# Two transformer blocks on one core: the expert gather spread over the stages of the second mixer

## The chip, the cores and the metric

One core of one Trainium2 chip runs the whole program. The metric is device time in microseconds, the median of repeated executions. Everything is float32 in memory, 512 tokens, model width 1024.

## The reference

Two blocks follow each other on `x`. Each is a token mixer and then a PEER feed-forward, in which every token picks 128 rows (8 heads, 16 each) of two tables of 16384 experts:

```python
def peer_ffn(h, ...):
    s1, s2 = scores of the two halves of q = h @ w_query against 128 keys each
    v1, i1 = top_k(s1, 16); v2, i2 = top_k(s2, 16)
    top_v, pos = top_k(v1[:, None] + v2[None, :], 16)      # 16 of 256
    expert_idx = i1 * 128 + i2 at pos;  gates = softmax(top_v)
    act = gelu(einsum('d,kd->k', h, expert_down[expert_idx]))
    return einsum('k,kd->d', gates * act, expert_up[expert_idx])

def second_block(x, mem, ...):
    h = rmsnorm(x); z = h @ w_in                           # 47 chunks of 128 columns
    o_fox = causal attention, 8 heads of 64, with a forget term cumsum(log_f) over all tokens before
    o_swa = window attention, 8 heads of 64, window 128, ALiBi, sinks
    o_mem = attention to 256 memory rows, 4 heads of 128   # keys and values from mem alone
    merged = sum of sigmoid(gates_i) * (o_i @ w_o_i)
    x = x + merged @ w_out
    x = x + peer_ffn_2(rmsnorm(x))
```

The second mixer of a token reads that token's `x` after the first feed-forward, and keys and values of the tokens before it, never after it.

## The kernel before

The program is a sequence of stages, each a block in which every engine has its own instruction list; at the end of a block all engines meet at a barrier. Activations lie feature-major in SBUF (`xT`, `hT`: 128 x 8 x 512). The order inside a stage is written by hand, with semaphores; nothing is scheduled by a planner.

- **First mixer** (from the start to about 1005 us), untouched but for the layout of two weights. Then norm `n2` and `peer` for the first feed-forward ("e1").
- **`peer`** (L1230) is `project_stage` for the queries (`e1q`, 16 chunks) and `sparse_stage` (L1050 on). `project_stage` (L261) takes a chunk of weights (512 KB), splits it on ACT and DVE into a high and a low part, and makes 24 products of 128x128 by all the tokens on TensorE. Two weight buffers, four PSUM banks.
- **`sparse_stage`**: for a tile of 128 tokens DVE chooses the experts in 21 pieces (`choose`, L1158). The gather then runs over 512 **slots**, 4 tiles of 128 experts. For a slot POOL issues one indirect DMA (L1064) of 128 rows of 8 KB, the down row and the up row of one expert per token side by side (1 MB) into one of 8 `pair` buffers. DVE takes the dot product of the down half with `hrow` (L1219). After every 4 slots ACT takes gelu (`bent`), DVE multiplies by the gate (`weight`), ACT makes a diagonal matrix per slot (`diag`, L1131), and TensorE adds `diag` times the up half into two banks (L1101, L1102). A buffer is free when TensorE is done (`added`), and POOL waits for that before it issues the slot that is 8 later. The choosing of tile t+1 is spread over the slots of tile t; that of tile 0 stands alone ahead of the gather.
- **Second mixer** (`second_mixer`, L1373), all 512 tokens at once, nothing beside it: norm `n3`; projection `p2` of 47 chunks; head norms `hn`; `forget`; `vt` (values turned); the attentions `foxa`, `swaa` (with a load of ALiBi first), the memory path (`mn`, `mp`, `mh`, `mt`) and `mema`; `mg2` (`merge_stage`, L960); `po2`; norm `n4`.
- **Second feed-forward** ("e2"), the same as the first: queries, choosing of tile 0, 512 slots, and the store of `xT`.

`attention_stage` (L502) works item by item (a head and a tile of queries): TensorE scores, DVE takes the peak, ACT exponentiates, DVE scales, TensorE turns, ACT copies, TensorE weighs the values, DVE takes the output, each a step or more behind the other, with 3 PSUM banks for scores and 2 for outputs. `norm_stage` (L224), `head_norm_stage` (L1238), `turn_stage`, `forget_stage` are short chains over ACT, TensorE and DVE. What sets the order around the change:

```python
for n in range(N):                                   # POOL, sparse_stage
    t, s = divmod(n, NJ)
    if s == 0:
        pool.wait_ge(chosen, t + 1)
    if n >= BUFS:
        pool.wait_ge(added, n - BUFS + 1)
```

Of the kernel before, what the change touches and what calls it, by code (L numbers as in the profile page):

```python
# [14 lines left out]
P = 128  # L15
S = 512
# [19 lines left out]
Y_FQ, Y_FK, Y_FV, Y_SQ, Y_SKV, Y_MQ, Y_GATE, Y_FF, Y_N = 0, 4, 8, 12, 16, 18, 22, 46, 47  # L36
# [138 lines left out]

class AdaBeside:
# [47 lines left out]
def norm_stage(nc, name, k, src, chunks, width, gain, dst, shift=None, tokens=S):  # L224

    with ExitStack() as stack:
# [4 lines left out]
        with nc.Block() as block:  # L231
            @block.scalar
            def _(act):
                for c in range(chunks):
                    act.activation(sq[:, c, :], src[:, c, :], ACT.Square).then_inc(sq_ready, 1)
                act.wait_ge(mean_ready, 1)
                act.activation(root[:], mean[:], ACT.Sqrt).then_inc(root_ready, 1)

            @block.tensor
            def _(pe):  # L240

                for c in range(chunks):
                    pe.wait_ge(sq_ready, c + 1)
                    last = pe.matmul(ss[:, 0:tokens], k.ones[:], sq[:, c, :], start=c == 0, stop=c == chunks - 1)
                last.then_inc(ss_ready, 1)

            @block.vector
            def _(dve):
                link = Chain(dve, chain)
                dve.wait_ge(ss_ready, 1)  # L250
# [3 lines left out]
                for c in range(chunks):  # L254
                    ins = dve.scalar_tensor_tensor(dst[:, c, :], src[:, c, :], gain[:, c:c + 1], rstd[:], ALU.mult, ALU.mult)
                    if shift is not None:
                        link(ins)
                        dve.tensor_scalar(dst[:, c, :], dst[:, c, :], shift[:, c:c + 1], None, ALU.add)


def project_stage(nc, name, k, w_dram, act_in, kc, chunks, dst, tokens=S, add=None, parts=None, ada=None):  # L261
# [4 lines left out]

    with ExitStack() as stack:
        r = Room(nc, stack, name)
        hhi, hlo = parts or (r.sb("hhi", [P, kc, tokens], F32R), r.sb("hlo", [P, kc, tokens], F32R))
# [4 lines left out]
        turns = (chunks - 1) // 4  # L274
# [12 lines left out]
        with nc.Block() as block:  # L287
            @block.sync
# [11 lines left out]
            def _(act):  # L300
# [7 lines left out]
                loop(act, body)  # L308

            @block.tensor  # L310
            def _(pe):
                def body(n, q, i):
# [9 lines left out]
                    if beside and q == 3 and i is not None:  # L322
                        beside.product(pe, i)

# [7 lines left out]
            def _(dve):  # L332
# [4 lines left out]
                def body(n, q, i):  # L337
                    if not (isinstance(n, int) and n == chunks - 1):
                        split_w(n + 1, q + 1)
                    if beside and i is not None:  # L340
                        beside.sums(dve, i, q)
                    dve.wait_ge(made, n + 3)
# [17 lines left out]
                if beside:  # L360
                    beside.finish(dve)

# [139 lines left out]
def attention_stage(nc, name, k, items, heads, vdim, oT, sinks=None):  # L502
# [5 lines left out]
    N = len(items)  # L508
    with ExitStack() as stack:
# [5 lines left out]
        ps = [r.ps(f"ps{u}") for u in range(3)]  # L515
        pt = [r.ps(f"pt{u}") for u in range(2)]
        po = [r.ps(f"po{u}") for u in range(2)]
# [3 lines left out]
        with nc.Block() as block:  # L521
            @block.tensor
            def _(pe):
                def score(n):
                    q_ap, k_ap, more = items[n][0], items[n][1], items[n][6]
                    if n >= 3:
                        pe.wait_ge(exped, n - 2)
                    out = ps[n % 3][:, 0:width[n]]
# [13 lines left out]
                def weigh_values(n):  # L542
                    vs, at = items[n][3], (items[n][4] % per) * vdim
                    pe.wait_ge(copied, n + 1)
                    if n >= 2:
                        pe.wait_ge(taken, n - 1)
                    for j, v in enumerate(vs):
                        last = pe.matmul(po[n % 2][at:at + vdim, 0:P], v, pT[n % 2][:, j * P:(j + 1) * P],
# [3 lines left out]
                for step in range(N + 3):  # L552
# [4 lines left out]
                    if 3 <= step:  # L557
                        weigh_values(step - 3)

            @block.scalar  # L560
            def _(act):
                for step in range(N + 2):
                    if step < N:
# [4 lines left out]
                        act.activation(p[n % 3][:, 0:width[n]], ps[n % 3][:, 0:width[n]], ACT.Exp, bias=nmax[:, n:n + 1],  # L568
# [5 lines left out]
                    if step >= 2:  # L574
# [4 lines left out]
                        act.activation(pT[n % 2][:, 0:width[n]], pt[n % 2][:, 0:width[n]], ACT.Copy).then_inc(copied, 1)  # L579

            @block.vector
            def _(dve):
                link = Chain(dve, chain)
                masked = [0]

                def peak(n):
# [3 lines left out]
                    if bias is not None:  # L590
                        part = ps[n % 3][:, w - bias.shape[-1]:w]
# [1012 lines left out]
```

## Time and profile before

| | |
|---|---|
| median of 3 runs | 5064.99 us (5050.13 to 5074.23) |
| the profiled execution: its time, its span | 5070.55 us, 5068.7 us |
| busy: PE, DVE, ACT, POOL | 75%, 54%, 16%, 23% of the span |
| DMA | 1194.16 MB, of them 1073.81 MB by the gather's queue |
| first gather, second gather | 1170 to 2607 us, 3627 to 5062 us |
| between them (second mixer, queries, choosing of tile 0) | 2607 to 3627 us |

The profile gives busy time per engine, a picture of the span in 40 slices, the costliest groups of instructions (line, engine, operation, tiles written and read, count, busy time, mean, idle time before them and what ended it), and DMA sizes with the time from issue to landing. Tile names have their buffer numbers left out. A float32 product on TensorE shows as two records. The granted clock is given as a share of 2.4 GHz: 1.00 is 2.4 GHz, 0.50 is 1.2 GHz.

### The profile page before, as it was taken

The page shows a single profiled execution, that of the slowest core. Times are in us where ns is not written, and L with a number is a line of the kernel's source. Part 1 is how long each engine was busy: PE and PEld are TensorE (multiplying, and loading weights), DVE is VectorE, ACT ScalarE, POOL GpSimd, SP SyncE. Part 2 cuts the span into 40 slices and gives each one's busy share as a digit, 9 for nine tenths or more (in the row PEclk, how much of TensorE's full clock was granted, in tenths as well). Part 3 has the DMA queues.
Part 4 walks back from the last instruction along what each step waited for, and adds up shares of the span by engine and source line. Part 5 has one row for each costly group of instructions (what it writes and reads, how often), then busy time and mean ns, then how long its engine had stood idle before and what let it go on. Part 6 is the DMA issues. An engine that isn't in the chain of part 4 may idle for free. (4 is left out here: it accounts for less than half of the span.)

```text
span 5068.7 us, 35703 instructions
## 1 busy us (share of the span) xinstructions
PE 3812.7 (75%) x11658; PEld 2123.6 (42%) x11658; DVE 2712.9 (54%) x5846; ACT 813.6 (16%) x2074; POOL 1174.9 (23%) x1028
## 2 busy tenths in 40 slices
PE   5945897775677777677779979788477777777777
PEld 4823796462233233233338734546223332322333
DVE  5558555346655656644443334533665565565454
ACT  1113001111111111111121212322111111111111
POOL 0000000002443444344410000000144334434443
PEclk9978787887888998888889955699788888988898
DMA  4500000127999999999952200122399999999998
GB/s 173 181 16 3 4 1 21 56 64 282 366 376 368 369 393 368 360 387 395 394 212 95 73 1 9 42 75 75 147 365 363 387 352 373 383 357 381 400 414 344
DMA packets 198993, 1194.16 MB, mean 236 GB/s; under 512 B 21642, under 2 KB 44426, under 8 KB 64914
## 3 DMA queue, kind: packets, MB, share of 16 engines
q0 software_dynamic: 147456, 1073.81, 53.3%
q1 hardware_dynamic: 51124, 118.42, 7.1%
q8 instruction: 76, 1.25, 0.1%
q14 instruction: 81, 0.66, 0.0%
q10 hardware_dynamic: 256, 0.02, 0.0%
HBM read 1190.04 MB, written 2.10 MB: 235 GB/s over the span
## 5 line engine op out<-in xcount | busy, mean ns | idle before, releaser
L1064 POOL DMA_INDIRECT e1g_pair<-in_experts,e1g_expert x512 | 585.7, 1144 | 1997.7 <-DVE e1g_expert L1196 1169.8
L1064 POOL DMA_INDIRECT e2g_pair<-in_experts,e2g_expert x512 | 589.0, 1150 | 1865.9 <-DVE e2g_expert L1196 1043.4
L1219 DVE CUSTOM_DVE_ANT_0 e2g_pair<-e2g_pair,e2g_hrow 128x1024 f32<-128x1024 f32 x512 | 626.4, 1225 | 601.6 <-DMA e2g_pair<-in_experts,e2g_expert 601.2
L1219 DVE CUSTOM_DVE_ANT_0 e1g_pair<-e1g_pair,e1g_hrow 128x1024 f32<-128x1024 f32 x512 | 626.8, 1225 | 598.8 <-DMA e1g_pair<-in_experts,e1g_expert 598.1
L1101 PE MATMUL e1g_acc<-e1g_pair,e1g_diag 128*128 128x512 f32 x1024 | 616.7, 688 | 425.2 <-ACT e1g_diag L1131 425.0
L1101 PE MATMUL e2g_acc<-e2g_pair,e2g_diag 128*128 128x512 f32 x1024 | 618.5, 689 | 422.7 <-ACT e2g_diag L1131 422.4
L1102 PE MATMUL e1g_acc<-e1g_pair,e1g_diag 128*128 128x512 f32 x1024 | 579.9, 651 | 0.0
L1102 PE MATMUL e2g_acc<-e2g_pair,e2g_diag 128*128 128x512 f32 x1024 | 579.0, 650 | 0.0
L1101 PEld LDWEIGHTS e1g_acc<-e1g_pair,e1g_diag 128*128 128x128 f32 x1024 | 210.1, 217 | 743.5 <-ACT e1g_diag L1131 460.1
L1101 PEld LDWEIGHTS e2g_acc<-e2g_pair,e2g_diag 128*128 128x128 f32 x1024 | 210.1, 217 | 739.6 <-ACT e2g_diag L1131 456.6
L1102 PEld LDWEIGHTS e2g_acc<-e2g_pair,e2g_diag 128*128 128x128 f32 x1024 | 219.2, 214 | 294.5 <-issue 294.5
L1102 PEld LDWEIGHTS e1g_acc<-e1g_pair,e1g_diag 128*128 128x128 f32 x1024 | 218.6, 213 | 293.3 <-issue 293.3
L318 PE MATMUL p_ps<-p_hhi,p_whi 128*128 128x512 f32 x648 | 255.4, 394 | 38.8 <-DVE p_wlo L335 38.8
L319 PE MATMUL p_ps<-p_hlo,p_whi 128*128 128x512 f32 x648 | 254.0, 392 | 0.0
L320 PE MATMUL p_ps<-p_hhi,p_wlo 128*128 128x512 f32 x648 | 253.9, 392 | 0.0
L1125 ACT ACTIVATE e2g_bent<-e2g_dot 128x4 f32<-128x4 f32 x128 | 26.3, 205 | 1053.8 <-DVE e2g_dot L1219 1053.8
L1125 ACT ACTIVATE e1g_bent<-e1g_dot 128x4 f32<-128x4 f32 x128 | 26.3, 205 | 1052.8 <-DVE e1g_dot L1219 1052.8
L1131 ACT ACTIVATE e1g_diag<-held_ident,e1g_weight 128x128 f32<-128x128 f32 x512 | 163.6, 390 | 165.0 <-DVE e1g_weight L1225 164.8
L1131 ACT ACTIVATE e2g_diag<-held_ident,e2g_weight 128x128 f32<-128x128 f32 x512 | 163.6, 390 | 164.8 <-DVE e2g_weight L1225 164.6
L345 DVE COPY mix_z<-p_ps 128x512 f32 (+1 forms) x81 | 56.0, 691 | 232.4 <-PE p_ps L320 232.4
L318 PEld LDWEIGHTS p_ps<-p_hhi,p_whi 128*128 128x128 f32 x648 | 122.8, 190 | 65.8 <-issue 40.5
L304 ACT ACTIVATE p_whi<-p_raw 128x1024 fp32r<-128x1024 f32 x81 | 85.8, 1061 | 352.8 <-PE p_ps L320 349.0
(515 smaller groups left out, 4704.5 us busy)
## 6 DMA issues: line engine op xcount, KB each, us to landing
p_raw<-in_w_in SPq DMA_DIRECT2D x81, 512.0 KB, 3.5
p_w_ada<-in_w_ada SPq DMA_DIRECT2D x16, 1024.0 KB, 6.1
ada_w<-in_w_ada SPq DMA_DIRECT2D x4, 2048.0 KB, 10.6
po_raw<-in_w_out SPq DMA_DIRECT2D x16, 512.0 KB, 3.6
e1q_raw<-in_w_query SPq DMA_DIRECT2D x16, 512.0 KB, 3.5
e1g_pair<-in_experts,e1g_expert POOLq DMA_INDIRECT x512, 9.0
e2q_raw<-in_w_peer_q SPq DMA_DIRECT2D x16, 512.0 KB, 3.5
e2g_pair<-in_experts,e2g_expert POOLq DMA_INDIRECT x512, 8.9
```

The lines of the kernel that those rows point to most:

```text
L304: act.activation(whi[q % 2][:], raw[q % 2][:], ACT.Copy).then_inc(w_hi, 1)
L318: pe.matmul(out, hi, hhi[:, c, :], start=c == 0, stop=False)
L319: pe.matmul(out, hi, hlo[:, c, :], start=False, stop=False)
L320: last = pe.matmul(out, lo, hhi[:, c, :], start=False, stop=c == kc - 1)
L345: ins = dve.tensor_copy(row(dst, n), got)
L1064: pool.indirect_dma_start(pair[n % BUFS][:], None, table, bass.IndirectOffsetOnAxis(ap=expert[:, t % 2, s:s + 1], axis=0)).then_inc(landed ...
L1101: pe.matmul(acc[0][:], diag[n % DIAGS][:], pair[n % BUFS][:, D:D + 512], start=s == 0, stop=s == NJ - 1)
L1102: pe.matmul(acc[1][:], diag[n % DIAGS][:], pair[n % BUFS][:, D + 512:2 * D], start=s == 0, stop=s == NJ - 1).then_inc(added, 1)
L1125: act.activation(bent[:, t % 2, at], dot[:, t % 2, at], gelu).then_inc(bent_made, 1)
L1131: act.activation(diag[n % DIAGS][:], k.ident[:], ACT.Copy, scale=weight[:, t % 2, s:s + 1]).then_inc(diag_made, 1)
L1219: ins = dve.tensor_tensor_reduce(pair[n % BUFS][:, 0:D], pair[n % BUFS][:, 0:D], hrow[:, t, :], 1.0, 0.0, ALU.mult, ALU.add, dot[:, t % 2, ...
```

## The change

The gather of both layers becomes one object, `Gather`, that lives through both feed-forwards and the second mixer. Its work is written as **beats**: at beat n POOL issues the down rows of slot n+6 and the up rows of slot n-15, DVE takes the dot of slot n, ACT makes `diag` of slot n-20, TensorE adds slot n-21. Down and up rows come from two tables, by two gathers of 128 rows of 4 KB (512 KB each), into 6 buffers of each kind; a down buffer is free after the dot, an up buffer after TensorE. Gelu and gate are taken for 16 slots at a time, not 4.

Every stage from then on takes `beats` and, on each engine, puts its share of the beats between its own instructions. The tokens go by halves of 256: tiles 0 and 1 of layer 1 (beats 0 to 283) run beside the choosing of tiles 1 to 3 and the memory path, whose keys and values are parked in DRAM; then half 0 goes through the second mixer, its queries and the choosing of its first tile beside 223 beats of tiles 2 and 3 (283 to 506); the choosing of its second tile stands beside 33 beats (506 to 539); half 1 goes through the same beside 223 beats of layer 2, tiles 4 and 5 (539 to 762); its last choosing stands beside 48 beats, and `drain_stage` runs the other 241. Projections that host beats are written out flat and not as a loop, `w_in_2`, `w_out_2`, the output weights of the branches and `w_peer_q` are read once per half, the projection to gates (`pg`, 24 chunks) is split from that to the heads (`p2`, 23 chunks), and attention has 2 banks for scores and 1 for outputs. Keys, values and the running forget sum of half 0 are kept (`Past`).

```diff
+GROUP, UBUFS, VBUFS, DIAGS = 16, 6, 6, 8
+BENT_AT = GROUP + 1
+WEIGH_AT = BENT_AT + 1
+DIAG_AT = WEIGH_AT + 2
+UP_AT = DIAG_AT + 1
+BEATS = SLOTS + UP_AT + 6
+class Gather:
+    def pool(self, pool, n):
+        for m in range(0 if n == 0 else n + UBUFS, n + UBUFS + 1):
+            if m < SLOTS:
+                t, s = divmod(m, NJ)
+                if s == 0:
+                    pool.wait_ge(self.chosen, t + 1)
+                if m >= UBUFS:
+                    pool.wait_ge(self.dotted, m - UBUFS + 1)
+                pool.indirect_dma_start(self.down[m % UBUFS][:], None, self.layers[t // TT][0],
...
+        m = n - UP_AT + VBUFS
+        if 0 <= m < SLOTS:
+            t, s = divmod(m, NJ)
+            if m >= VBUFS:
+                pool.wait_ge(self.added, m - VBUFS + 1)
+            pool.indirect_dma_start(self.up[m % VBUFS][:], None, self.layers[t // TT][1],
...
+    def pe(self, pe, n):
+        m = n - UP_AT
+        if 0 <= m < SLOTS:
+            t, s = divmod(m, NJ)
+            pe.wait_ge(self.up_in[m % VBUFS], 16 * (m // VBUFS) + 16)
+            pe.wait_ge(self.diag_made, m + 1)
...
+class Beats:
+    def at(self, i):
+        return range(self.first + i * self.count // self.points, self.first + (i + 1) * self.count // self.points)
...
-def project_stage(nc, name, k, w_dram, act_in, kc, chunks, dst, tokens=S, add=None, parts=None, ada=None):
+def project_stage(nc, name, k, w_dram, act_in, kc, chunks, dst, tokens=S, add=None, ada=None, beats=None):
...
-        turns = (chunks - 1) // 4
+        turns = 0 if hosting else (chunks - 1) // 4
...
+                    if hosting:
+                        beats.pe(pe, n)
...
+                    if hosting:
+                        beats.dve(dve, n)
                     dve.wait_ge(made, n + 3)
...
+    SC, PO = (2, 1) if hosting else (3, 2)
...
-        ps = [[r.ps(f"ps{i}_{u}") for u in range(2)] for i in range(nb)]
+        ps = [r.ps(f"ps{u}") for u in range(5)]
...
+MIXER_LENGTHS = {"n3": 15, "p2": 100, "hn": 40, "vt": 8, "forget": 15, "foxa": 110, "swaa": 70, "mema": 30, "pg": 110, "mg": 70, "po": 35,
+                 "n4": 15, "q": 70, "choose": 90}
...
+        beats = shared_out(gather, 0, half_done, {"choose1": 62, "mn": 8, "mp": 50, "mh": 12, "mt": 4, "choose": 144})
...
+    starts = [half_done, first_layer_done]
+    ends = [TT * NJ - UBUFS, (TT + HTILES) * NJ - UBUFS]
+    for half in range(2):
+        t = TT + HTILES * half
+        beats = shared_out(gather, starts[half], ends[half], MIXER_LENGTHS)
+        second_mixer(nc, k, ins, cols, past, xT, hT, memory, half, beats)
...
+            project_stage(nc, f"e2qh{half}", k, ins["w_peer_q"], h, DC, 2 * PH, qT, tokens=HALF, beats=beats["q"])
...
+    drain_stage(nc, gather, Beats(gather, ends[1] + 48, BEATS))
```

How the order of instructions moves, at three places. POOL in the middle of a gather, before (`e1g_pair` are the buffers of 8 KB rows, `e1g_expert` the chosen indices):

```order
L1064 DMA e1g_pair2<-in_experts1,e1g_expert 128x2048 [waits e1g_added]
L1064 DMA e1g_pair3<-in_experts1,e1g_expert 128x2048 [waits e1g_added]
L1064 DMA e1g_pair4<-in_experts1,e1g_expert 128x2048 [waits e1g_added]
L1064 DMA e1g_pair5<-in_experts1,e1g_expert 128x2048 [waits e1g_added]
L1064 DMA e1g_pair6<-in_experts1,e1g_expert 128x2048 [waits e1g_added]
```

And after the change:

```order
L221 DMA held_up1<-in_up1,held_expert 128x1024 [waits held_added]
L214 DMA held_down5<-in_down1,held_expert 128x1024 [waits held_dotted]
L221 DMA held_up2<-in_up1,held_expert 128x1024 [waits held_added]
L214 DMA held_down0<-in_down1,held_expert 128x1024 [waits held_dotted]
L221 DMA held_up3<-in_up1,held_expert 128x1024 [waits held_added]
L214 DMA held_down1<-in_down1,held_expert 128x1024 [waits held_dotted]
```

POOL issues two gathers where it issued one, half of them waiting for DVE's dot and half for TensorE.

TensorE in the fox attention, before (`foxa_ps` scores, `foxa_pt` turned weights, `foxa_po` outputs; all heads and tiles, one item after another):

```order
L529 MATMUL foxa_ps2<-mix2_z 128x512
L531 MATMUL foxa_ps2<-fox_fk,held_hT 128x512
L539 MATMUL foxa_pt1<-held_ident,foxa_p0 128x128 x2
L548 MATMUL foxa_po0<-foxa_pT0,local_v 64x128
L529 MATMUL foxa_ps0<-mix2_z 128x128
L531 MATMUL foxa_ps0<-fox_fk,held_hT 128x128
```

And after (half 0):

```order
L743 MATMUL foxah0_ps1<-foxh0_fk,foxh0_fq 128x128
L751 MATMUL foxah0_pt1<-held_ident,foxah0_p1 128x128 x2
L760 MATMUL foxah0_po0<-foxah0_pT0,held_v 64x128 x2
L241 MATMUL held_acc0<-held_up2,held_diag6 128x512
L242 MATMUL held_acc1<-held_up2,held_diag6 128x512
L241 MATMUL held_acc0<-held_up3,held_diag7 128x512
L242 MATMUL held_acc1<-held_up3,held_diag7 128x512
L741 MATMUL foxah0_ps0<-held_fox_k,partsh0_z 128x256
L743 MATMUL foxah0_ps0<-foxh0_fk,foxh0_fq 128x256
```

One or two slots of the gather stand between two steps of the attention.

DVE inside a gather of the kernel before, where a group of four dots ends in one product with the gates:

```order
L1219 ISA e1g_pair0,e1g_dot<-e1g_pair0,e1g_hrow 128x1024
L1219 ISA e1g_dot 128x1
L1219 ISA e1g_pair1,e1g_dot<-e1g_pair1,e1g_hrow 128x1024
L1219 ISA e1g_dot 128x1
L1219 ISA e1g_pair2,e1g_dot<-e1g_pair2,e1g_hrow 128x1024
L1219 ISA e1g_dot 128x1
L1219 ISA e1g_pair3,e1g_dot<-e1g_pair3,e1g_hrow 128x1024
L1219 ISA e1g_dot 128x1
L1225 TENSOR_TENSOR e1g_weight<-e1g_bent,e1g_gate 128x4
```

And DVE in the gate projection of half 0 after the change (`pgh0_wlo` the low part of a weight chunk, `mix2h0_z` its result):

```order
L539 COPY mix2h0_z<-pgh0_ps1 128x256
L527 TENSOR_TENSOR pgh0_wlo1<-pgh0_raw1,pgh0_whi1 128x1024
L286 ISA held_down0,held_dot<-held_down0,held_hrow 128x1024
L286 ISA held_dot 128x1
L539 COPY mix2h0_z<-pgh0_ps2 128x256
L527 TENSOR_TENSOR pgh0_wlo0<-pgh0_raw0,pgh0_whi0 128x1024
L286 ISA held_down1,held_dot<-held_down1,held_hrow 128x1024
L286 ISA held_dot 128x1
L286 ISA held_down2,held_dot<-held_down2,held_hrow 128x1024
```

A dot, which waits for its gather, now stands ahead of the copy that frees a bank of the projection.

## Rows read from the trace of the kernel before

**Rows 1.** The page's picture of the span in 40 slices

```profile
PE   5945897775677777677779979788477777777777
PEclk9978787887888998888889955699788888988898
DMA  4500000127999999999952200122399999999998
```

**Rows 2.** Busy time by stage: window, its length, then as the first line says

```profile
core 0: us, PE busy (x) PEld busy (x) DVE busy (x) ACT busy (x) POOL busy (x), PEclk, DMA share, GB/s
1107.00:1170.00 63.00, 9.77 (x64) 8.61 (x64) 52.98 (x210) 7.22 (x11) 0.00 (x0) 0.61 0.01 3
1170.00:2607.00 1437.00, 1057.60 (x2176) 443.15 (x2176) 807.68 (x1811) 202.81 (x658) 585.67 (x512) 0.87 0.94 374
...
2620.00:2890.00 270.00, 255.36 (x1115) 211.22 (x1116) 101.63 (x110) 53.95 (x55) 0.00 (x0) 0.96 0.29 91
2890.00:2950.00 60.00, 47.69 (x83) 15.93 (x81) 22.32 (x44) 11.21 (x18) 0.00 (x0) 0.69 0.02 5
2950.00:2974.00 24.00, 4.50 (x20) 4.13 (x20) 10.22 (x12) 4.45 (x5) 0.00 (x0) 0.50 0.01 1
2974.00:3126.00 152.00, 150.21 (x368) 75.01 (x368) 52.88 (x193) 31.73 (x97) 0.00 (x0) 0.50 0.00 0
...
3137.00:3216.00 79.00, 77.22 (x223) 41.73 (x223) 57.03 (x238) 29.02 (x119) 0.00 (x0) 0.50 0.00 1
...
3241.00:3266.00 25.00, 24.85 (x192) 24.58 (x192) 11.66 (x15) 6.47 (x7) 0.00 (x0) 0.93 0.41 127
...
3284.00:3306.00 22.00, 20.24 (x119) 14.96 (x117) 16.42 (x70) 12.70 (x43) 0.00 (x0) 0.97 0.01 1
3306.00:3405.00 99.00, 87.49 (x200) 39.47 (x201) 34.85 (x50) 21.25 (x35) 0.00 (x0) 0.93 0.27 80
...
3563.00:3627.00 64.00, 9.95 (x64) 8.78 (x64) 52.27 (x209) 7.22 (x11) 0.00 (x0) 0.60 0.05 17
```

**Rows 3.** Waits inside the first gather (total us, times, longest)

```profile
POOL e1g_pair L1064 <- PE e1g_acc L1102: 800.3, 433, 11.3
DVE e1g_pair L1219 <- DMA e1g_pair<-in_experts,e1g_expert: 598.1, 455, 6.1
```

**Rows 4.** Timeline, first gather at full clock: start, length, what

```profile
2300.97 1.23 DVE L1219 CUSTOM_DVE_ANT_0 e1g_pair<-e1g_pair,e1g_hrow 128x1024 f32<-128x1024 f32 x1 [1.22 <-DMA e1g_pair<-in_experts,e1g_expert]
2301.37 1.02 PE L1101 MATMUL e1g_acc<-e1g_pair,e1g_diag 128*128 128x512 f32 x2
...
2302.12 0.08 DVE L1219 DVE_READ_ACCUMULATOR2_ANT e1g_dot<- 128x1 f32 x1
...
2303.09 1.02 PE L1101 MATMUL e1g_acc<-e1g_pair,e1g_diag 128*128 128x512 f32 x2
...
2303.44 1.23 DVE L1219 CUSTOM_DVE_ANT_0 e1g_pair<-e1g_pair,e1g_hrow 128x1024 f32<-128x1024 f32 x1 [1.23 <-DMA e1g_pair<-in_experts,e1g_expert]
...
2303.53 1.95 POOL L1064 DMA_INDIRECT e1g_pair<-in_experts,e1g_expert  x1 [0.52 <-PE e1g_acc L1102]
```

**Rows 5.** Timeline, POOL at the start of the first gather

```profile
1174.12 0.93 POOL L1064 DMA_INDIRECT e1g_pair<-in_experts,e1g_expert  x1 [0.30 <-issue]
```

**Rows 6.** The page's groups: count, busy us, mean ns, idle before

```profile
L1064 POOL DMA_INDIRECT e2g_pair<-in_experts,e2g_expert x512 | 589.0, 1150 | 1865.9 <-DVE e2g_expert L1196 1043.4
L1219 DVE CUSTOM_DVE_ANT_0 e2g_pair<-e2g_pair,e2g_hrow 128x1024 f32<-128x1024 f32 x512 | 626.4, 1225 | 601.6 <-DMA e2g_pair<-in_experts,e2g_expert 601.2
```

**Rows 7.** DMA issues: count, KB each, median us from issue to landing

```profile
p_raw<-in_w_in SPq DMA_DIRECT2D x81, 512.0 KB, 3.5
p_w_ada<-in_w_ada SPq DMA_DIRECT2D x16, 1024.0 KB, 6.1
e1g_pair<-in_experts,e1g_expert POOLq DMA_INDIRECT x512, 9.0
```

**Rows 8.** Busy time in the first mixer's attention, columns as in rows 2

```profile
384.00:445.00 61.00, 54.15 (x294) 34.04 (x293) 48.18 (x178) 28.61 (x90) 0.00 (x0) 1.00 0.00 1
```

More of the change, by code:

```diff
@@ L176, with shared_out @@
+def shared_out(gather, first, last, lengths):
+    whole, run, got = sum(lengths.values()), 0, {}
+    for name, length in lengths.items():
+        a, run = run, run + length
+        got[name] = Beats(gather, first + (last - first) * a // whole, first + (last - first) * run // whole)
+    return got
 class AdaBeside:
@@ L499, in _, with attention_stage @@
                 dve.tensor_copy(kk[:, :, :, NOPE:QH], bcast(kr[:], MH, 2)).then_inc(heads, 1)
-def attention_stage(nc, name, k, items, heads, vdim, oT, sinks=None):
+def attention_stage(nc, name, k, items, heads, vdim, oT, sinks=None, loads=(), beats=None):
     per = P // vdim
     N = len(items)
+    hosting = beats is not None
+    SC, PO = (2, 1) if hosting else (3, 2)
+    apart = PO == 2 or all(items[n][4] % per != items[n + 1][4] % per for n in range(N - 1))
+    beats = (beats or Beats()).over(N + 4)
     with ExitStack() as stack:
@@ L1228, in _ @@
[L1228 to L1239 removed]
+                        link(dve.tensor_tensor(gather.gate[:, t % TT, :].rearrange("p (h n) -> p h n", h=PH), tv[:], bcast(total[:], K16, 2), ALU.mult))
@@ new lines, in choose, with drain_stage, _ @@
+                        link.announce(dve.scalar_tensor_tensor(gather.expert[:, t % TT, :], found[:, 0, :], float(NK), found[:, 1, :], ALU.mult, ALU.add), gather.chosen, t + 1)
+                dve.wait_ge(loaded, 32)
+                for j, (t, _) in enumerate(tiles):
+                    for i in range(PIECES):
+                        choose(j, t, i)
+                        beats.dve(dve, PIECES * j + i)
+def drain_stage(nc, gather, beats):
+    beats = beats.over(1)
+    with nc.Block() as block:
+        @block.gpsimd
+        def _(pool):
+            beats.pool(pool)
+            gather.settle(pool)
+        @block.tensor
+        def _(pe):
+            beats.pe(pe, 0)
+        @block.scalar
+        def _(act):
+            beats.act(act, 0)
+        @block.vector
+        def _(dve):
+            beats.dve(dve, 0)
@@ L1245, in head_norm_stage @@
+def head_norm_stage(nc, name, row_pick, chunks, tokens=S, beats=None):
     N = len(chunks)
+    beats = (beats or Beats()).over(2 * N)
     with ExitStack() as stack:
@@ L1293, in _ @@
                 ins.then_inc(ones_ready, 1)
-                for n, (_, gain, _, times) in enumerate(chunks):
+                for n, (_, gain, _, times, _) in enumerate(chunks):
                     ins = dve.tensor_scalar(gains[:, n:n + 1], gain, times, None, ALU.mult)
                 link(ins)
+                for n in range(N):
+                    beats.dve(dve, n)
                 dve.wait_ge(summed, N)
```

601 lines of the change are left out of this document (369 added, 232 removed).

## Prediction

> **What bounds the kernel now.** I read the picture of the span first. DMA stands at nine tenths in two blocks of slices and at nought to three between them, and TensorE is at seven tenths or more in nearly all slices from the first gather on [rows 1]. So the two gathers are limited by moving rows, and the second mixer between them by something else. The busy times by stage say by what: a gather moves 374 GB/s with DMA at 0.94 [rows 2], 1437 us for 512 slots, 2.81 us a slot, while the projection `p2` keeps TensorE busy 255 of 270 us with DMA at 0.29. The waits inside the gather show the ring at work: POOL waits 800 us for TensorE to free a `pair` buffer, and DVE waits 598 us for rows to land [rows 3]. In the timeline rows land every 2.47 us when the queue is full (dots at 2300.97 and 2303.44), and TensorE takes 1.72 us a slot at full clock (2301.37 to 2303.09) [rows 4]. From the first gather's start (1170 us) to the end, TensorE has about 1024 x 1.72 = 1760 us of gather work and DMA at least 1024 x 2.47 = 2530 us, beside 1020 us in which nothing is gathered (2607 to 3627). The change puts these side by side. What it can win is at most that 1020 us, less what the two then cost each other.
>
> **The change part by part.** I cost the program by its stages, since beats are dealt out to stages and no stage can borrow from another: a stage takes the longest of TensorE, DVE and POOL on its own work and its beats.
>
> *POOL.* It issues 2048 gathers and not 1024. One takes 0.93 to 0.94 us, and 0.30 us pass to the next, when nothing disturbs it [rows 5], 1.24 in all. The mean is 1.15 [rows 6]: the gather at 2303.53 took 1.95 and ended 0.81 after the end of the dot that ran beside it (2303.44 + 1.23) [rows 4], so an issue that meets a running dot waits for its end. With as many dots per slot and twice the issues the mean should hold: 1.15 + 0.30 = 1.45 us an issue, 2.90 a slot. That is more than the 2.81 of now. The bound below is 1.24, where dots and issues fall into step (the rows' landing rate, 2.47 / 2, allows it too); I take 1.45, a mean over 512 issues.
>
> *DMA.* The same bytes in half the piece. A row of 4 KB in a gather is not in this trace. The nearest rows are loads of 512 KB and 1 MB, alone, 3.5 and 6.1 us to landing [rows 7]: two for one is 7.0 to 6.1, 15% more. But a gather takes 9.0 us to land while rows land every 2.47, so the fixed part is hidden by those in flight, and 12 of the new pieces are in flight. I take no cost, and 15% as the other end. The page "DMA: Bandwidth & Descriptors" of the Trainium skill (Bandwidth) says to batch to 1 MiB or more for 75% of peak, and fits one DMA as 2.0 us plus bytes by 436 GB/s: 4.4 us for 1 MiB, 6.4 for two halves, which would make a slot 4.1 us, an estimate. By that, the sum below would be about 5380. The trace speaks against it, as gathers overlap.
>
> *Weights twice.* 71 chunks of 512 KB and the output weights go once per half. At half of 3.5 us each [rows 7], as two are under way at a time, they are some 125 us per half, in stages in which TensorE sets the time; with 223 x 2.47 = 551 us of rows that is 676, below the 884 found next. No cost; were TensorE not the bound, DMA would be late next.
>
> *A mixer half.* TensorE's own work for 256 tokens: a chunk is 25 / 8 = 3.1 us (the memory projection, 8 chunks of 256 tokens) against 5.7 for 512 (270 / 47) [rows 2]. So `p2` 23 chunks 72, `pg` 75, queries 16 chunks 50, `po` 25. The attentions ran at 1.2 GHz (0.50 granted) though TensorE was busy 150 of 152 us [rows 2]; the first mixer's ran at 1.00 [rows 8]. With full 128x128 products of the gather for over half of the time I take full clock: `foxa` 152 us, halved for the tokens and halved for the clock, 38, `swaa` 20, `mema` 10; merge 87 x 0.93 / 2 = 41; head norms 48 x 0.69 / 2 = 17. The beats are dealt by the table, 223 / 778 = 0.287 a unit, at 1.72 us each on TensorE: `p2` 28.7 beats 49, `hn` 20, `foxa` 31.5 beats 54, `swaa` 34, `mema` 15, `pg` 54, merge 34, `po` 17, queries 34. Sums, with 3 to 5 us for a stage's start and end and more where a step's chain runs over three engines: `p2` 125, `pg` 133, queries 88, `po` 46, `foxa` 105, `swaa` 68, `mema` 35 (its keys come back from DRAM first), merge 80, `hn` 38; the norms 14 each, `vt` 8, `forget` 25 of the 24 it and `vt` now take together (small moves beside full queues). Choosing is DVE's: 63 us for 53 busy [rows 2], and 25.8 beats x 1.31 (a dot of 1.225 [rows 6] and its read of 0.08 [rows 4]) = 34, with the keys' load 105. In all **884 us a half**. POOL's 223 x 2.90 = 647 is hidden under it.
>
> *The rest.* Until beat 283 POOL issues 289 down and 268 up gathers, 557 x 1.45 = 808; the choosing of three tiles (190 us of DVE with the chains) and the memory path (68 us before, between 3216 and 3284) are hidden under that, with 12 us for two loads that host no beats. The choosing of tile 5: 63 + 33 x 1.31 = 106, say 110. From beat 762 on 256 down and 277 up gathers are left, 533 x 1.45 = 773, and 20 us for the last group of 16 on TensorE, the turning and the store. A projection written out flat, the norm's extra branches, barriers of blocks that were there before: no cost, hidden by TensorE's queue; the new layouts of output weights and five banks in the merge lie where DMA is at 0.27 [rows 2], no cost or gain.
>
> *Sum.* 1170 + 808 + 12 + 884 + 110 + 884 + 773 + 20 = **4661 us** of span, against 5068.7, so 408 less. The profiled execution took 5070.55 us, 0.1% over the median of 5065. I forecast 4660 for the median.
>
> **The rivals.** *A, POOL in step.* If issues take 1.24 us, the 1090 issues that lie where POOL sets the time cost 0.21 less each: 4430. For it: the down gather is issued right after a dot ends. Against: the up gather follows it and meets the next dot.
>
> *B, the slow clock stays.* If `foxa` and `swaa` still run at 1.2 GHz, they take 184 and 108 us, 119 more a half: 4900. For it: products with 64 rows and with 2 rows stay among the work, and 0.50 was granted at 99% busy.
>
> *C, small pieces cost.* 15% on 2.81 is 3.23 us a slot, 1.61 an issue: 1090 x 0.16 = 175 more, 4835. The skill's rule names a larger price, given above, and shares this case's chance.
>
> *D, the other side: lockstep.* The engines' lists are in order. A dot that waits for its rows holds the copy behind it that frees a bank; TensorE then waits at the next chunk, its own slots come late, `added` comes late, and POOL issues late. If this goes round, hosted work and gather add and do not overlap. A half then takes of its own half of 888 (2607 to 3563 without the memory path), 15 for products at 256 tokens and 64 for choosing, and 647 of gather, 1170; tile 5 takes 160, tile 7 64 more, and the first phase 257 more: 5600. It decides from the point where 410 of these 940 us are lost, an overlap under 56%. For it: one bank for outputs, two for scores, six buffers, and the last wait named for DVE in the gather is DMA [rows 3]. Against: in mixer stages TensorE needs 5.3 us for a chunk and its 1.25 slots, and POOL only 3.6, so rows should lie ready.
>
> *E, nothing.* The order lists show the beats in every stage, so the change does what it says; gains and losses could still cancel.
>
> **How the numbers follow.** The forecast has 0.55, A 0.11, B 0.10, C 0.08, D 0.13, E 0.03. A measurement of this kernel tells about 0.5% from no change. Faster is forecast, A, B and C and a part of D with partial overlap: 0.86; within 0.5% 0.03; slower 0.11. The forecast's own spread is the stage starts and chains, some 30 us in each half and 0.1 us on 1090 issues, 4530 to 4800. The range takes in A and B, 4430 to 4940, and leaves out D, E and tails of A and B.
>
> **What would show it.** In the changed profile: no stretch with DMA under half from 1170 us on; POOL's gathers at 1.1 to 1.2 us mean and 2.9 us a slot in the drain; each mixer half near 884 us with TensorE over 85% busy; a clock near 1.00 in `foxa`; the first phase ended near 1990 us. If POOL's idle time before a gather in the drain is long and ended by DMA landing through DVE, C is right; if in `p2` TensorE waits for the low part or for rows in every chunk, D is. The prediction is wrong if the halves are not near 884 or the drain is not near 2.9 a slot.

## The result, and the profile after

The changed kernel takes 5109 us (median of 5 runs, 5105.24 to 5115.27) against 5071 for the kernel before on the same chip (5 runs, 5050.13 to 5084.15): a ratio of 1.0082, 95% interval 1.0054 to 1.0109. It is slower by 0.8%, where 4660 us was forecast, and lies outside the range of 4430 to 4940. The profiled execution has a span of 5113.4 us, 452 above the sum of 4661.

The page's picture of the span of the changed kernel, to be laid beside [rows 1]:

```profile
PE   5945898773585676697689675697879685677777
POOL 0000000005665777555544356554544346777775
PEclk9977787887897999898899898898989898899999
DMA  4500000117896999787788777786778777899998
```

The hole of [rows 1] is gone: from slice 10 on DMA is at six tenths or more everywhere, so the gathers do run beside the mixer. But DMA is at seven and eight tenths where the gathers of before had nine, and TensorE, which the sum held to be over 85% busy in the mixer halves, is often at six or seven. The busy times by stretch say the same (core 0; window, its length, then PE, PEld, DVE, ACT and POOL busy with their instructions, granted clock, DMA share, GB/s). The stretches are the first phase, half 0 up to its queries, the choosing of tiles 4 and 5, half 1 up to its queries, and the end, each from block end to block end:

```profile
1173.00:2108.00 935.00, 583.79 (x1392) 238.61 (x1392) 527.22 (x1277) 123.63 (x329) 650.12 (x557) 0.89 0.88 320
2108.00:3011.00 903.00, 713.76 (x3106) 457.49 (x3106) 467.31 (x968) 230.17 (x533) 434.57 (x394) 0.89 0.80 280
3011.00:3250.00 239.00, 133.82 (x324) 57.34 (x324) 174.96 (x548) 28.64 (x75) 150.20 (x118) 0.86 0.77 268
3250.00:4179.00 929.00, 741.60 (x3226) 469.13 (x3226) 477.29 (x963) 238.79 (x533) 425.94 (x394) 0.89 0.78 272
4179.00:5113.00 934.00, 636.06 (x1340) 235.86 (x1340) 460.19 (x1019) 122.74 (x343) 649.82 (x585) 0.94 0.90 333
```

Forecast were 820, 779, 215, 779 and 898 (each half of 884 less its choosing of 105, which goes with tile 5's 110). So every stretch is too long (by 115, 124, 24, 150 and 36), most of all those with many stages. Yet *inside* a stage nothing is wrong. The same view inside `p2`, `foxa` and `pg` of half 0, `foxa` of half 1, and the end:

```profile
2140.00:2254.00 114.00, 114.00 (x658) 87.34 (x656) 66.87 (x102) 31.71 (x51) 62.87 (x54) 0.99 0.93 339
2364.00:2452.00 88.00, 84.87 (x253) 37.68 (x252) 58.23 (x155) 25.74 (x82) 67.27 (x55) 0.98 0.91 315
2606.00:2731.00 125.00, 125.00 (x708) 94.83 (x707) 75.20 (x119) 34.73 (x57) 69.38 (x61) 0.98 0.92 341
3511.00:3619.00 108.00, 107.31 (x350) 47.77 (x348) 63.88 (x155) 32.36 (x82) 62.25 (x56) 1.00 0.77 259
4480.00:5050.00 570.00, 405.50 (x813) 139.85 (x812) 251.05 (x418) 74.73 (x214) 426.66 (x402) 0.98 0.97 369
```

TensorE is busy for 114 of 114 us, 125 of 125, 107 of 108; the clock is at its upper level, 2.4 GHz, in the attentions too, and the end issues 402 gathers in 570 us, 2.84 us a slot. Lockstep (D) and the slow clock (B) cannot be seen. The time must lie where stages meet. The timeline over the end of `p2` and the start of `hn` in half 0 (start, length, what, idle before and its releaser):

```profile
2253.51 1.02 PE L242 MATMUL held_acc<-held_up,held_diag 128*128 128x512 f32 x2
...
2254.34 0.94 POOL L214 DMA_INDIRECT held_down<-in_down,held_expert  x1 [0.30 <-issue]
2255.58 0.94 POOL L221 DMA_INDIRECT held_up<-in_up,held_expert  x1 [0.30 <-issue]
2263.94 0.25 SPq L1426 DMA_DIRECT2D hnh_pick<-in_row_pick  x1
2263.95 0.73 ACT L1433 ACTIVATE hnh_sq<-partsh_z 128x256 f32<-128x256 f32 x2 [19.97 <-PEq L466]
2264.02 0.19 DVE L1460 MEMSET hnh_ones<- 128x68 f32 x2 [12.45 <-PEq L466]
...
2264.59 2.77 PE L1445 MATMUL hnh_mean<-hnh_sq,hnh_ones 128*34 128x256 f32 x6 [10.06 <-DVE hnh_ones L1466]
...
2267.11 1.68 POOL L214 DMA_INDIRECT held_down<-in_down,held_expert  x1 [10.59 <-DVE held_dot L286]
```

POOL's last gather of the block is issued at 2256.52. Then no engine does anything until 2263.9, when all start together. The releaser named is the sequencer at the barrier. The trace has one instruction on POOL in that time, a DRAIN from 2254.58 to 2263.69, which no view of the page counts as busy. The windows around it, the last 8 us of `p2`, the gap and the 8 us behind it:

```profile
2246.50:2254.50 8.00, 8.00 (x37) 4.81 (x35) 3.13 (x6) 0.00 (x0) 3.82 (x5) 1.00 0.74 247
2256.50:2263.70 7.20, 0.00 (x0) 0.00 (x0) 0.00 (x0) 0.00 (x0) 0.02 (x1) 0.68 0.48 170
2263.70:2272.00 8.30, 7.33 (x17) 2.61 (x17) 7.82 (x34) 3.29 (x9) 3.12 (x2) 0.66 0.33 92
```

In the gap only DMA works, at 170 GB/s, and it moves the gathers that were in flight. Behind it the gather's buffers have to fill again (92 GB/s). Of such block ends the changed kernel has 36 from the first gather on (6, 13, 2, 13 and 2 in the five stretches). At none of the 36 is a packet of the gather's queue still moving when the DRAIN ends; the last one has ended 0.5 to 4.6 us before (2.7 us here). POOL stands in its drain alone for 4.8 to 10.0 us each time, 240 us in all, and all engines idle for 292 us at these ends. In the kernel before the same DRAIN takes 0.03 us at its block ends in the second mixer, where nothing is in flight.

POOL's groups of the page, which answer to [rows 6], and the waits of the end stretch (4480 to 5050; total us, times, longest), which answer to [rows 3]:

```profile
L214 POOL DMA_INDIRECT held_down<-in_down,held_expert x1024 | 1140.3, 1114 | 2196.1 <-SPq L1271 1172.6
L221 POOL DMA_INDIRECT held_up<-in_up,held_expert x1024 | 1170.4, 1143 | 583.9 <-PE held_acc L242 351.3
```

```profile
PEld held_acc L241 <- DMA held_up<-in_up,held_expert: 288.1, 175, 3.2
DVE held_down L286 <- DMA held_down<-in_down,held_expert: 285.3, 179, 4.4
...
POOL held_down L214 <- issue: 61.3, 201, 0.3
POOL held_up L221 <- issue: 38.1, 125, 0.3
POOL held_up L221 <- PE held_acc L242: 25.9, 68, 3.0
```

A gather takes POOL 1.114 and 1.143 us, as forecast (1.15). In the end stretch POOL is busy 427 of 570 us, 99 more are its step of 0.30 us between issues, it waits 26 for TensorE, and the profile puts 18 down as remote; TensorE and DVE wait for rows to land. Whether the rows are late because DMA is full (0.97) or because POOL issues them late, this view does not tell. The runs e10 and e11 below bear on it.

**Theory 1:** the drain at block ends that now have gathers in flight takes the expected gain. **Rivals:** the meeting of the engines itself, which breaks the pipeline of slots; small pieces (C); lockstep (D).

### The profile page after: what moved, and what is told of

Its sections match the earlier page's. It is cut to its first block and busy times, and to the rows that moved or that the text cites. A ratio compares the mean times of both kernels' runs of the same rounds, so it can differ in the third digit from the quotient of the medians.

```text
span 5113.4 us, 42808 instructions
## 1 busy us (share of the span) xinstructions
PE 3666.9 (72%) x13654; PEld 2134.7 (42%) x13654; DVE 2766.4 (54%) x5954; ACT 919.0 (18%) x2092; POOL 2310.9 (45%) x2052
## 5 line engine op out<-in xcount | busy, mean ns | idle before, releaser
L214 POOL DMA_INDIRECT held_down<-in_down,held_expert x1024 | 1140.3, 1114 | 2196.1 <-SPq L1271 1172.6
L286 DVE CUSTOM_DVE_ANT_0 held_down<-held_down,held_hrow 128x1024 f32<-128x1024 f32 x1024 | 1240.0, 1223 | 715.2 <-DMA held_down<-in_down,held_expert 567.9
L241 PE MATMUL held_acc<-held_up,held_diag 128*128 128x512 f32 x2048 | 1152.6, 645 | 588.9 <-DMA held_up<-in_up,held_expert 476.2
L221 POOL DMA_INDIRECT held_up<-in_up,held_expert x1024 | 1170.4, 1143 | 583.9 <-PE held_acc L242 351.3
L242 PE MATMUL held_acc<-held_up,held_diag 128*128 128x512 f32 x2048 | 1084.1, 612 | 0.0
L241 PEld LDWEIGHTS held_acc<-held_up,held_diag 128*128 128x128 f32 x2048 | 337.0, 195 | 1136.3 <-DMA held_up<-in_up,held_expert 882.0
L242 PEld LDWEIGHTS held_acc<-held_up,held_diag 128*128 128x128 f32 x2048 | 402.5, 197 | 516.6 <-issue 516.6
L266 ACT ACTIVATE held_diag<-held_ident,held_weight 128x128 f32<-128x128 f32 x1024 | 361.8, 393 | 1017.5 <-PE held_acc L242 420.1
L508 PE MATMUL pgh_ps<-pgh_hhi,pgh_whi 128*128 128x256 f32 x384 | 128.5, 335 | 32.5 <-DVE pgh_wlo L527 32.5
L508 PE MATMUL p_ps<-p_hhi,p_whi 128*128 128x512 f32 x272 | 107.6, 396 | 21.5 <-DVE p_wlo L527 21.5
L509 PE MATMUL p_ps<-p_hlo,p_whi 128*128 128x512 f32 x272 | 106.5, 392 | 0.0
L510 PE MATMUL p_ps<-p_hhi,p_wlo 128*128 128x512 f32 x272 | 106.4, 391 | 0.0
```

What stands on the lines that cost most here:

```text
L214: pool.indirect_dma_start(self.down[m % UBUFS][:], None, self.layers[t // TT][0], bass.IndirectOffsetOnAxis(ap=self.expert[:, t % TT, s:s ...
L221: pool.indirect_dma_start(self.up[m % VBUFS][:], None, self.layers[t // TT][1], bass.IndirectOffsetOnAxis(ap=self.expert[:, t % TT, s:s + ...
L241: pe.matmul(self.acc[0][:], diag[:], up[:, 0:512], start=s == 0, stop=s == NJ - 1)
L242: pe.matmul(self.acc[1][:], diag[:], up[:, 512:D], start=s == 0, stop=s == NJ - 1).then_inc(self.added, 1)
L266: act.activation(self.diag[m % DIAGS][:], self.k.ident[:], ACT.Copy, scale=self.weight[:, t % 2, s:s + 1]).then_inc(self.diag_made, 1)
L286: dve.tensor_tensor_reduce(down[:], down[:], self.hrow[:, t % TT, :], 1.0, 0.0, ALU.mult, ALU.add, self.dot[:, t % 2, s:s + 1]).then_inc(s ...
```

## The experiments

**e1: no drain of POOL at a block's end.** Everywhere:

```diff
-        with nc.Block() as block:
+        with nc.Block(no_gpsimd_drain=True) as block:
```

> Every block ends with its barrier, but without POOL's DRAIN, which waits for the gathers in flight. Theory 1 (the drains): in the changed kernel POOL's DRAIN stands last at 35 block ends after the first gather starts, 6.6 us each after all other engines have come, some 235 us in all, and the queue has to fill again after each. Without it the time falls by 200 to 300 us, to 4810 to 4910. Theory 2 (the boundary itself): the engines would wait for one another there anyway, as each must reach the same beat; then less than 60 us goes, to 5050 or more. Theory 3 (small pieces of 512 KB and a static order): the same as theory 2, nothing goes.

Measured: 4806 us (4789.33 to 4825.69), ratio to before 0.9462 (0.9436 to 0.9489), 303 less than the changed kernel. The same five stretches (to be laid beside those above), and the same block end (the 10 us ahead of it, the end itself, the 8 behind):

```profile
1173.00:2042.00 869.00, 576.30 (x1392) 236.32 (x1392) 527.86 (x1278) 124.44 (x328) 629.29 (x550) 0.93 0.92 338
2042.00:2854.00 812.00, 716.82 (x3106) 457.28 (x3106) 467.46 (x968) 229.98 (x533) 445.38 (x401) 0.92 0.88 316
2854.00:3070.00 216.00, 129.79 (x325) 55.74 (x324) 174.96 (x549) 28.79 (x76) 146.63 (x113) 0.92 0.80 281
3070.00:3906.00 836.00, 742.77 (x3226) 468.75 (x3226) 477.46 (x963) 238.31 (x533) 433.29 (x401) 0.93 0.86 307
3906.00:4823.00 917.00, 637.67 (x1340) 236.01 (x1340) 460.42 (x1019) 122.82 (x343) 647.10 (x587) 0.95 0.92 341
```

```profile
2165.00:2175.00 10.00, 10.00 (x60) 7.62 (x58) 6.58 (x9) 2.77 (x6) 4.52 (x5) 1.00 0.93 354
2175.00:2182.00 7.00, 6.56 (x33) 4.19 (x31) 1.72 (x5) 0.03 (x1) 4.08 (x4) 1.00 0.72 236
2182.00:2190.00 8.00, 7.23 (x21) 2.51 (x22) 7.12 (x32) 3.55 (x10) 4.90 (x4) 1.00 0.79 262
```

TensorE's busy time in half 0 is 717 us as before the edit (714); the stretch is 91 us shorter at 13 block ends, 7.0 us each. The others give 66, 23, 93 and 17, so 290 us in all, close to the 292 us in which all engines idled. At the end of `p2` TensorE is busy 6.56 of 7 us, and POOL issues through it. The version is 5.4% faster than the kernel before.

**e2: eleven more block ends,** with the drain, in the last 241 beats:

```diff
-    drain_stage(nc, gather, Beats(gather, ends[1] + 48, BEATS))
+    for i in range(11):
+        drain_stage(nc, gather, Beats(gather, ends[1] + 48 + 20 * i, ends[1] + 68 + 20 * i), last=False)
+    drain_stage(nc, gather, Beats(gather, ends[1] + 268, BEATS))
```

> The changed kernel with the 241 last beats, which run with nothing beside them, cut into 12 blocks by 11 more boundaries (with the DRAIN). Theory 1: each costs the drain of the gathers in flight, 5 to 7 us, and the refilling, so 6 to 10 us each and 70 to 110 us in all, 5180 to 5220. Theory 2 and 3: the engines are a beat apart, so 1 to 3 us each, under 35 us in all.

Measured: 5196 us (5192.90 to 5199.95), ratio 1.0241 (1.0219 to 1.0263): 87 over the changed kernel by the medians (81 by the two ratios), **7.3 to 7.9 us for a block end**. In the trace all engines idle for 80 us at the eleven.

**e6: the same eleven, without the drain** (e2's edit on e1).

> The changed kernel with POOL's drain left out at its block ends, and with the same eleven further block boundaries in the last 241 beats as before. Theory 1 (what a boundary costs is POOL's drain, which waits for the gathers in flight): without it a boundary costs about what it costs with no gather in flight, 1 us or less, so at most 15 us over the 4806 of the version without drains: 4806 to 4821. Rival (the boundary itself, the meeting of the engines, breaks the pipeline of slots): again about 7.9 us each, 4806 + 87 = 4893.

Measured: 4797 us (4796.04 to 4798.80), ratio 0.9461 (0.9434 to 0.9489). Eleven more block ends cost nothing that can be measured. So the meeting of the engines costs nothing here, and the drain is the cost.

**e7: the kernel before without the drain** (e1's edit on it).

> Control: the kernel before with POOL's drain left out at its block ends. Theory 1: no gather is in flight at those ends that matter, the drain there takes 0.03 us, so within 15 us of the kernel before, about 5060. Rival (the drains cost something of their own at any block end, and the 303 us are a gain that has nothing to do with the change): faster by 100 us or more, under 4970.

Measured: 5081 us (5059.12 to 5090.92), ratio 1.0021 (1.0000 to 1.0042): nothing gained. The 303 us are a cost that the change brought, and no gain that the kernel before could have had.

**e5: no overlap.** The beats of each half stand in a block of their own ahead of it, and the mixer half runs bare:

```diff
-        beats = shared_out(gather, starts[half], ends[half], MIXER_LENGTHS)
+        drain_stage(nc, gather, Beats(gather, starts[half], ends[half]), last=False)
+        beats = shared_out(gather, ends[half], ends[half], MIXER_LENGTHS)
```

> The changed kernel with the 223 beats of each mixer half run in a block of their own ahead of it, and no beats in the half. If the overlap in the halves is worth what the forecast gave it (gather 223 x 2.85 = 635 and about 480 of its own against 908 to 934 measured with beats), the time rises by 2 x 190 = 380, to about 5490, less the drains that are no longer there (14 a half at 5 to 8 us, 170 in all), so about 5320. If hosting gives nothing (lockstep, rival D of the forecast), it stays within 50 of the changed kernel or falls.

Measured: 5496 us (5473.86 to 5503.73), ratio 1.0826 (1.0789 to 1.0862): 387 over the changed kernel, and 176 over the 5320 that was expected. In its trace 10 block ends with gathers in flight are left of 36, so the time of 26 drains is gone as expected; the overlap that was given up was worth more than the 380 us that the expectation gave it. The next run prices it without drains.

**e8: no overlap and no drain** (e5's edit on e1).

> The beats of each half in a block of their own ahead of it, and POOL's drain left out. Theory 1 (the overlap works, and its gain was given back by the drains): against the 4806 of the version with overlap and without drains, the two halves of the mixer alone take 502 + 534 = 1036 us and 446 beats at 2.85 take 1271, together 2307, against the 823 + 847 = 1670 that they took together: 637 slower, about 5440; against the version with drains (5496) 40 to 60 less, since few boundaries have gathers in flight. Rival (lockstep: the overlap hides little, the drains are only part of it): within 300 us of 4806.

Measured: 5397 us (5385.53 to 5414.65), ratio 1.0638 (1.0604 to 1.0671), 591 over e1. Its gather alone ahead of half 0, its two bare halves, and `foxa` in the first of them:

```profile
2040.00:2665.00 625.00, 447.60 (x884) 155.10 (x882) 273.22 (x460) 80.98 (x233) 455.67 (x439) 0.96 0.97 367
2673.00:3175.00 502.00, 401.16 (x2310) 334.67 (x2310) 238.63 (x554) 151.16 (x308) 6.57 (x7) 0.78 0.32 102
3986.00:4531.00 545.00, 448.05 (x2431) 352.94 (x2430) 250.03 (x555) 159.71 (x308) 6.50 (x7) 0.77 0.30 95
...
2816.00:2867.00 51.00, 50.53 (x136) 27.02 (x134) 23.09 (x95) 12.70 (x49) 0.00 (x0) 0.50 0.00 1
```

A slot alone takes two issues, 2 x 625 / 439 = 2.85 us. Half 0 takes 502 us bare and 812 with 197 beats in it (e1), so a slot beside the mixer costs 310 / 197 = 1.57 us; in half 1 it is (836 - 545) / 197 = 1.48. That is below the 1.72 us of TensorE that the prediction counted for a slot, since a part of it falls into time in which TensorE idled in the bare half (101 of 502 us). So the overlap works, and lockstep falls.

**e3: the kernel before, each slot's rows in two gathers of 4 KB a row.** Nothing else changes:

```diff
-                    pool.indirect_dma_start(pair[n % BUFS][:], None, table,
-                                            bass.IndirectOffsetOnAxis(ap=expert[:, t % 2, s:s + 1], axis=0)).then_inc(landed[n % BUFS], 16)
+                    for part in range(2):
+                        pool.indirect_dma_start(pair[n % BUFS][:, part * D:(part + 1) * D], None, table[part],
+                                                bass.IndirectOffsetOnAxis(ap=expert[:, t % 2, s:s + 1], axis=0)).then_inc(landed[n % BUFS], 16)
```

> The kernel before with the two rows of a slot gathered by two DMAs of 512 KB from two tables into the same pair buffer, nothing else. It prices the small pieces by themselves. If they are hidden: within 30 us of before. If the packets set the pace (the profiles show 181 ns for 4 KB in the changed kernel against 329 ns for 8 KB before, so 2.9 us of DMA a slot against 2.64): 2.81 becomes about 3.0 us a slot, 1024 x 0.2 = 200 us more, 5270. If the issues on POOL add (1.45 us each, after the wait for TensorE): up to 3.2 us a slot, 5450.

Measured: 5278 us (5275.53 to 5287.04), ratio 1.0407 (1.0383 to 1.0431), 210 slower, 0.205 us a slot. That is a price of the two pieces, but of the rows or of the issues? The number is that of the expectation's packets (5270); the next run shows that it can come without them.

**e11: the kernel before, with 8 KB rows as they are and a second gather of 64 bytes a row for each slot.**

```diff
+                    pool.indirect_dma_start(small[n % BUFS][:], None, table[1],
+                                            bass.IndirectOffsetOnAxis(ap=expert[:, t % 2, s:s + 1], axis=0)).then_inc(landed[n % BUFS], 16)
```

> The kernel before, whose gathers stay at 8 KB a row, with a second gather of 64 bytes a row issued for every slot: POOL issues 2048 and not 1024, the bytes grow by under 1%. Theory POOL (the +210 us of the kernel before with its rows in two pieces is the pace of POOL's issues): again 150 to 250 slower, 5220 to 5320. Theory DMA (it is the price of rows of 4 KB): POOL's issues are hidden, and only 131072 small packets are added, 5070 to 5140.

Measured: 5260 us (5237.89 to 5270.49), ratio 1.0367 (1.0331 to 1.0403), 194 slower. POOL's groups in the first gather (1200 to 2600 us; count, busy, mean ns, idle before), of the kernel before and then of e11:

```profile
L1064 POOL DMA_INDIRECT e1g_pair<-in_experts,e1g_expert x501 | 574.2, 1146 | 815.5 <-PE e1g_acc L1102 790.0 <-issue 25.5
```

```profile
L1067 POOL DMA_INDIRECT e1g_small<-in_small,e1g_expert x476 | 541.0, 1136 | 145.2 <-issue 145.2
L1065 POOL DMA_INDIRECT e1g_pair<-in_experts,e1g_expert x475 | 514.0, 1082 | 200.2 <-issue 124.5 <-PE e1g_acc L1105 60.8 <-remote 14.9
```

A gather of 64 bytes a row takes POOL as long as one of 8 KB, and POOL's waiting for TensorE goes from 790 to 61 us. POOL is nearly full: 1055 us of issues and 270 us of steps between them, of 1400. With under 1% more bytes nearly all of e3's loss is there, so e3 needs no price of smaller rows.

**e10: e1 with rows of 2 KB for 4 KB,** half the bytes, the same issues, dots and products (the second half of each expert's rows is left out; the `up` rows likewise, and the buffers are filled with zeros once):

```diff
-                pool.indirect_dma_start(self.down[m % UBUFS][:], None, self.layers[t // TT][0],
+                pool.indirect_dma_start(self.down[m % UBUFS][:, :D // 2], None, self.layers[t // TT][0],
```

> The version without drains, with rows of 2 KB in place of 4 KB in every gather: the second half of each expert's down and up row is left out (the buffers hold zeros there), so the bytes of the gathers are halved, and POOL's issues, the dots and the products stay as they are. Twelve buffers are filled with zeros once, about 12 us. Theory POOL (in the gather-only stretches POOL's issue of 1.12 plus 0.30 sets the pace, 2.84 us a slot): the last stage stays near 900 us and the whole near 4800 (4760 to 4830). Theory DMA (moving 1 MB a slot in small rows sets it): a slot falls to 1.9 us or less, where TensorE or POOL alone would bound it; the last stage falls to 600 to 700 us, the whole to 4350 to 4500.

Measured: 4790 us (4779.52 to 4803.34), ratio 0.9442 (0.9418 to 0.9466). Half the bytes gain 16 us of 4806, and the intervals of the two overlap. The end stretch (4300 to 4750) of e10, and of e1:

```profile
4300.00:4750.00 450.00, 300.95 (x608) 104.43 (x607) 187.20 (x312) 55.47 (x159) 358.87 (x300) 0.99 0.63 175
```

```profile
4300.00:4750.00 450.00, 318.45 (x640) 110.64 (x640) 196.36 (x329) 58.95 (x169) 333.79 (x317) 0.98 0.97 369
```

At half the bytes DMA falls to 0.63, and still POOL issues no faster: 300 gathers against 317. POOL is full there, 359 us of issues and 300 steps of 0.30, and its issues have become longer: of 299, 149 last over 1.05 us, against 66 of 316 in e1, and each of these ends 0.8 us after the end of a dot, as the prediction read it from one gather [rows 4]. So POOL's two issues alone hold a slot at 2.8 to 3.0 us. That DMA would allow much less at 4 KB rows is not shown: in e1 it is at 0.97 of 2.84 us, so the two limits lie close together.

**e9: e1 with groups of 8 beats for 16** (`GROUP = 8`), so that issues stand nearer to their use.

> The version without drains with a group of 8 beats in place of 16 between an issue and its use (table loads of ScalarE twice as often). Theory 1 (issues start nearer their use, and no stage waits for the group): 4806 less up to 20 us. Rival (ScalarE's table loads for twice as many groups stand in the path): 4806 plus 10 to 60 us.

Measured: 4783 us (4768.85 to 4803.88), ratio 0.9424 (0.9390 to 0.9459). Its interval overlaps that of e1, so the 14 to 23 us are not shown to be a gain. No loss is shown either.

## Why the prediction was wrong

The books, by medians: doing the work by halves, without overlap and drains, costs 5397 - 5070 = 327 us; the overlap wins 5397 - 4806 = 591; the drains take 5109 - 4806 = 303. These three add up to the 38 us of the result by the way they are taken, so the sum is no check of its own. Of the first, the profiled executions (5412.6 against 5068.7, 344 more) say where it lies. The bare halves take 502 + 545 = 1047 us where the mixer before took 888 without the memory path, 159 more. Choosing the tiles 4 to 7 takes 398 us with 81 beats in it, where the kernel before takes 64 for tile 4 and 228 for 81 slots, 106 more. The other 79 are in the start and the stretches of gather. The 0.2 us a slot of e3 and e11 do not show in full here: the gather alone takes 2.85, against 2.81 before.

- **The step that failed:** "barriers of blocks that were there before: no cost, hidden by TensorE's queue". It was put at nothing without a row, and the kernel before could show no price, since its block ends have no gather in flight (0.03 us). The change moves the blocks over running gathers, and then the drain on POOL ends only after all have landed: 303 us, 8.4 at each of 36 ends (7.3 to 7.9 by e2). Shown by e1, e2, e6 and e7. No queue of TensorE's covers it, for it stops all engines. It is two thirds of the 452, and it alone turns faster into slower. Without it the profiled execution of e1 is 162 us above the sum, as follows.
- **Start, 1170 us:** 1173.
- **First phase, 820 us:** 869 without drains. An issue was to take 1.45 us and takes 1.56 (869 / 557). In a part of this stretch POOL's issues last longer, as its groups of the changed kernel from 1700 to 2080, where DVE chooses experts too, show (count, busy, mean ns):

```profile
L214 POOL DMA_INDIRECT held_down<-in_down,held_expert x125 | 163.2, 1306 | 43.9 <-issue 37.8 <-DVE held_dot L286 6.1
L221 POOL DMA_INDIRECT held_up<-in_up,held_expert x125 | 136.7, 1093 | 38.1 <-issue 31.1 <-PE held_acc L242 7.0
```

  Half of 1.306 + 1.093, and 0.30, is 1.50, of the 1.56. From 1350 to 1605 us in e1, beside the memory path, POOL also waits 19 us for DVE's dots and 15 for TensorE. The term was 6% too small, and the rows before could not have told: there an issue takes 1.14, 1.15 and 1.14 us in the three tiles that have choosing beside them and 1.15 in the one without. Why it is longer here was not isolated; the changed kernel puts the choosing of a tile beside 62 to 72 beats, where the kernel before has 128 slots.
- **A half up to its queries, 779 us:** 812 and 836 without drains, with 903 and 929 in the changed kernel. The mechanism held: the stages are TensorE's, which is busy 717 of 812 us. The sizes were off by 33 and 57. By stage in half 0 (without drains, from block end to block end): `p2` 127 for 125, `hn` 59 for 38, `foxa` 90 for 105, `swaa` 73 for 68, `mema` 42 for 35, `pg` 135 for 133, `merge` 87 for 80, `po` 52 for 46, queries 93 for 88. In half 1 `foxa` takes 111: it has 232 matmul records of its own where half 0 has 136, since attention is causal and later queries see more keys. The prediction had halved it evenly. For `hn` the clock counts too. It takes 59 us in e1 and 44 in e6, which has the same code up to there:

```profile
2182.00:2241.00 59.00, 57.05 (x116) 23.19 (x116) 25.64 (x67) 13.20 (x33) 24.56 (x25) 0.71 0.68 228
```

```profile
2177.00:2221.00 44.00, 42.19 (x116) 17.28 (x116) 25.22 (x67) 13.10 (x33) 24.14 (x24) 0.96 0.86 285
```

  Granted 0.71 and 0.96, for the same 116 products; TensorE is busy nearly throughout in both. Why the clock fell in one of them stays open.
- **Choosing, 105 + 110 us:** 216. **End, 773 + 20 + 105 us:** 917, 934 with drains. A slot takes 2.84 us there, near the 2.90 of the prediction's issue term.
- **Weights twice, small pieces, layouts: no cost.** No run takes the second reading of the weights or the layouts by themselves; TensorE is busy for 114 of 114 us in `p2` and 125 of 125 in `pg` above, so the weights do not hold it up there. For the small pieces e10 shows no clear gain from half the bytes.

Of the rivals, **A** (POOL in step, 1.24 an issue) is refused by 1.42 in the end stretch (570 / 402). **B** (the slow clock) is refused: `foxa` bare has 0.50 and beside the gather 0.98. **C** (small pieces cost) gave 4835, close to e1's 4806, but for another reason: C has the moving of small pieces as the cost, and in the kernel before the second issue alone costs 0.19 us a slot (e11), of which the sum had 0.09 (2.90 for 2.81). By the fit of the Trainium skill that the prediction weighed (the page "DMA: Bandwidth & Descriptors", Anatomy of one DMA), two halves would make a slot 4.1 us, an estimate; 2.84 was measured, so the trace does not agree with it for gathers of which several are in flight. **D** (lockstep) had the right side and the wrong mechanism: e8 against e1 shows 591 us of overlap, 295 a half, where the sum had 286 (D's 1170 less 884). **E** is refused, since the change does what it says.

## What to carry to other kernels

In the kernel before, the drain at a stage boundary cost nothing (e7), as nothing was in flight at it. Before moving one over DMAs that POOL has issued, ask what the boundary waits for: here each one let all the gathers land, 8 us, and the loss shows in no busy time, only as all engines idle at once with DMA running. Where correctness comes from semaphores on the landings, as here, leave the drain out or merge the blocks; with that the same change is 5% faster than the kernel before. And a gather has two prices, its bytes and its issue: splitting rows doubles the second, and here that brought POOL to its limit.

## What the runs showed of the hardware

- A DRAIN on POOL at a block's end took 7 to 19 us with gathers in flight, and ended 0.5 to 4.6 us after their last packet; with none in flight it took 0.03 us. Its time with POOL alone was 4.8 to 10.0 us.
- An indirect gather of 128 rows held POOL for 1.08 to 1.15 us on average and 0.30 to the next, whether a row has 64 bytes, 4 KB or 8 KB (1136, 1114 and 1146 ns). It took 0.94 us undisturbed; in the end stretches of e1 and e10 all 215 longer ones ended 0.8 us after the end of a dot on DVE.
- Rows of 2 KB moved 175 GB/s at a DMA share of 0.63 (e10), rows of 4 KB 369 at 0.97 (e1): 278 and 380 GB/s for a full share, by division. So rows of 2 KB took more DMA time for their bytes, but DMA had time to spare there; at 4 KB it had next to none.
- TensorE's clock in the attention was 0.50 (1.2 GHz) with TensorE busy 50.53 of 51 us, and 0.98 with products of 128x128 of the gather between (84.87 of 88 us busy).
